# Expert down-projection weights: their loads moved from ScalarE's DMA queue to SyncE's

## The chip, the cores and the metric

The kernel runs on one core of one Trainium2 chip. The metric is the device time of one execution in microseconds. TensorE (PE), VectorE (DVE), ScalarE (ACT), GpSimd (POOL) and SyncE (SP) each run their own instruction stream and meet only at semaphores. Transfers are issued from SP's queue (q1 in the profile), ACT's (q10) or POOL's (q0), and all of them are carried by the core's 16 DMA engines.

## The reference

The kernel computes a decoder trunk of two layers on 512 tokens of width 1024 in float32. Layer 0 mixes tokens by dilated window attention, layer 1 by a gated DeltaNet; each mixer is followed by a mixture of experts (MoE), and each sub-layer is modulated by `c` and closed by a layer norm. What the change touches is the MoE:

```python
def swiglu(x, w1, w3, w2):
    return (jax.nn.silu(x @ w1) * (x @ w3)) @ w2

# 64 experts of hidden width 256; each token takes its 8 best, plus one shared expert
scores = jax.nn.sigmoid(xt @ router_w)
...                                   # group-limited top-8 on scores + router_bias -> eidx
gates = scores[eidx] / sum * 2.5
for each expert e:                    # rows grouped by expert
    y = swiglu(x[tokens of e], w1[e], w3[e], w2[e])
    acc[tokens of e] += y * gate
out = acc + swiglu(xt, ws1, ws3, ws2)
```

Per layer an expert has w1 and w3 (1 MiB each, the up weights) and w2 (1 MiB, the down weights), so the 64 experts weigh 192 MiB, and every one of them is read once per layer.

## The kernel before, in words

`build` runs the stages one after the other: setup, attention, MoE of layer 0, DeltaNet, MoE of layer 1. The two MoE stages (`moe_stage`) are built by the same code and take about 590 us each, from 834 to 1424 us and from 2100 to 2690 us of the profile.

A MoE stage routes the tokens, ranks the experts by how many tokens chose them, and then works through 45 **passes** of 128 gathered rows. A pass holds the rows of one to three experts: the three fullest experts first, one pass each, then a fixed mixture of experts with 96, 128 and 64 rows (`expert_passes`, L772). An expert's weights are one **load**; loads are numbered 0 to 63 in the order in which the passes need them, and `last_pass[n]` is the last pass that uses load n. Passes 7, 8, 9 are the last ones of loads 7, of 8 and 9, and of 10 and 11; pass 10 is the first to need loads 12 and 13, pass 11 load 14, pass 12 load 15, pass 13 load 16.

PE's stream for pass p is: index rows of pass p+3 (`rows_of`, L1720), the up-projection of pass p+1 (`up_of`, L1734, out into `moe_ph` or `moe_pr`), transposes (L1697, L1709), the down-projection of pass p (`down_of`, L1748, out into `moe_py`). ACT copies the result out (L1199), POOL scatters it to `y_rows` in HBM (L1269) and gathers the token rows of pass p+3 (L1265). Before `rows_of` of the next pass DVE must have written the scatter indices (L1458), for which it waits until an earlier scatter has landed.

Weights are held in **slots**: five for up weights, four for down weights. The up weights of load n go into the slot that load n-5 used, so their transfer waits for the up-projection of `last_pass[n-5]` (semaphore `h_done`, counted up by PE after L1734). The down weights of load n go into the slot of load n-4 and have to wait for the down-projection of `last_pass[n-4]` (`y_done`, after L1748). Loads 0 to 2 come ahead of the passes.

Who issues them sets the order. SP's program issues the up weights of loads 3 to 63 in a row (L1076, each with its `h_done` wait; L860, two transfers of 1 MiB). ACT's program issues the down weights (L863, one transfer of 1 MiB): load 3 once the order of the experts is known, the rest after the two copies L1199 of the pass whose down-projection freed the slot, without a wait of their own:

```python
for n in range(ew.EARLY + 1, NE):
    if last_pass[n - len(ew.DOWN_SLOTS)] == p:
        load_down(n)
```

Of the kernel before, what the change touches and what calls it, by code (L numbers as in the profile page):

```python
# [43 lines left out]
NE, TOPK, NG, TOPG = 64, 8, 8, 4  # L44
# [8 lines left out]
class Stage:  # L53
# [11 lines left out]
    def sem(self, name):  # L65
        s = self.ctx.enter_context(self.nc.semaphore(f"{self.tag}_{name}"))
        self.sems.append(s)
        return s
# [734 lines left out]
class ExpertWeights:  # L803
# [54 lines left out]
    def load_up(self, sp, e, slot, done):  # L858
        for a, src in enumerate(self.up_dram):
            sp.dma_start(self.up_slot(slot, a), src[:, bass.ds(e, 1)].rearrange("p a n -> p (a n)")).then_inc(done, 16)  # L860
# [21 lines left out]
def moe_stage(nc, c, A, l, ada_rows, h_rows, y_rows, ew, ring=None, out=None):  # L882
# [6 lines left out]
    passes, load_rank, last_pass = expert_passes()  # L889
# [4 lines left out]
    w13, w2, rw, rb, w13_in, w2_in, router_in = ew.w13, ew.w2, ew.rw, ew.rb, ew.w13_in, ew.w2_in, ew.router_in  # L894
# [38 lines left out]
    order = st.sb("order", [1, NE], I32)  # L933
# [40 lines left out]
    def vector(t):  # L974
        return t[norm // 2, norm % 2]
# [7 lines left out]
    def on_partitions(v):  # L983
# [20 lines left out]
    kth_ready, kth_turned, kthT_ready, rank_ready, ranked_done, order_ready = [  # L1004
        sem(x) for x in "kth_ready kth_turned kthT_ready rank_ready ranked_done order_ready".split()]
# [6 lines left out]
    y_done, y_ready = sem("y_done"), sem("y_ready")  # L1012
# [30 lines left out]
    with nc.Block() as block:  # L1043
        @block.sync
        def _(sp):
            for m, v in ((G, vector(A["ln_g"])), (B, vector(A["ln_b"])), (SHIFT, part(0)), (SCALE, part(1))):
                sp.dma_start(cols[:, m], v.rearrange("(p k) -> p k", k=KT)).then_inc(cols_in, 16)
            ew.load_early(sp)
            def store(t):
                sp.wait_ge(xn_ready, t + 1)  # L1050
                sp.dma_start(h_rows[t * P:(t + 1) * P, :], c.x[:, t]).then_inc(ew.h_out, 16)

            for t in range(TT - 1):
                store(t)
            sp.wait_ge(o_done, 2 * TT)
            ew.load_expert(sp, 2)
            store(TT - 1)
            sp.wait_ge(o_used, 2 * TT)
            sp.dma_start(c.ada[:, 2], spread(part(2))).then_inc(gate_in, 16)
            if not final:  # L1060
                for m, v in ((G, after[0]), (B, after[1]), (SHIFT, ada_rows[mod + 1, 0:D]), (SCALE, ada_rows[mod + 1, D:2 * D])):
                    sp.dma_start(next_cols[:, m], on_partitions(v)).then_inc(next_cols_in, 16)
            sp.wait_ge(order_ready, 1)

            def expert(n):
                return sp.value_load(order[0:1, load_rank[n]:load_rank[n] + 1], min_val=0, max_val=NE - 1)

            def load_up(n, e):
                slot, times = ew.up_place(n)
                if times == 1:  # L1070
                    sp.wait_ge(s_up, TT)
                else:
                    sp.wait_ge(h_done, last_pass[n - len(ew.UP_SLOTS)] + 1)
                ew.load_up(sp, e, slot, w13_in[slot])

            for n in range(ew.EARLY, NE):  # L1076
                load_up(n, expert(n))
            sp.wait_ge(h_done, max(last_pass[n] for n in range(NE) if ew.up_place(n)[0] == 0) + 1)
            sp.dma_start(shared_down.rearrange("p k d -> p (k d)"), A["shared_w2"][l].rearrange("(p k) n -> p (k n)", k=2))\
                .then_inc(s_down_in, 16)  # L1080
            sp.wait_ge(y_done, PASSES)

            def block(j):
                r = sp.value_load(ovi[0:1, bass.ds(j, 1)], min_val=0, max_val=NE - 1)
                e = sp.value_load(order[0:1, bass.ds(r, 1)], min_val=0, max_val=NE - 1)
                ew.load_up(sp, e, SPARE_UP, ov["w"])
                ew.load_down(sp, e, SPARE_DOWN, ov["w"])
                sp.wait_ge(ov["out"], 16 * j + 16)
                sp.sem_inc(ov["turn"], 1)

            further(sp, block)
            for b in range(2):
                sp.wait_ge(y_out[b], 16 * ((PASSES + 1 - b) // 2))
            for m in range(TT * PAIRS):
                t, pair = m // PAIRS, m % PAIRS
                if t >= 2 and pair < ON_PE // YG:
                    sp.wait_ge(d_done, t - 1)
                elif t >= 2:
                    sp.wait_ge(yg_used, 3 * (t - 2) + (1, 3)[pair - ON_PE // YG])
                sp.dma_start(yg[m % NYG], y_rows.rearrange("(t p k) d -> p t k d", p=P, k=TOPK)[:, t, pair * YG:(pair + 1) * YG])\  # L1100
                  .then_inc(yg_in[m % NYG], 16)
            if final:
                for t in range(TT):
                    sp.wait_ge(out_ready, t + 1)
                    sp.dma_start(out[0, t * P:(t + 1) * P, :], c.x[:, t]).then_inc(x_out, 16)
                sp.wait_ge(x_out, 16 * TT)
            else:
                ring.load_early(sp)
                for n in range(ring.slots):
                    sp.wait_ge(ring.w_in[n], 16)  # L1110

        @block.scalar
        def _(act):
# [48 lines left out]
                act.wait_ge(tx_done, 2 * p + 2)  # L1162
                modulated(p % 2).then_inc(xT_act, 1)

            def load_down(n):
                e = act.value_load(order[0:1, load_rank[n]:load_rank[n] + 1], min_val=0, max_val=NE - 1)
                slot, times = ew.down_place(n)
                ew.load_down(act, e, slot, w2_in[slot])

            keep_hidden(0)  # L1170
            silu_shared(1)
            keep_hidden(1)
            act.wait_ge(order_ready, 1)
            load_down(ew.EARLY)
            silu_shared(2)
            turned(0)
            keep_hidden(2)
# [6 lines left out]
            for p in range(PASSES):  # L1184
                act.wait_ge(th_done, p + 1)
                nc.scalar.copy(hT2[:, p % 2], th[:]).then_inc(hT_ready, 1)  # L1186
                if p + 2 < PASSES:
                    turned(p + 2)
                if p + 1 < PASSES:
                    silu(p + 1)  # L1190
                if p == 26:
                    act.wait_ge(route_ready, 1)
                    for n in range(2):
                        act.dma_start(c.ada[:, n], spread(after[n])).then_inc(next_in, 16)
                if p >= 2:
                    act.wait_ge(y_out[p % 2], 16 * (p // 2))
                act.wait_ge(y_done, p + 1)
                for n in range(2):
                    nc.scalar.copy(ysb[:, p % 2, half(n)], py[n][:]).then_inc(y_ready, 1)  # L1199
                for n in range(ew.EARLY + 1, NE):  # L1200
                    if last_pass[n - len(ew.DOWN_SLOTS)] == p:
                        load_down(n)
            act.wait_ge(y_out[0], 16 * ((PASSES + 1) // 2))
            act.wait_ge(y_out[1], 16 * (PASSES // 2))

# [1334 lines left out]
```

## Time and profile before

| | |
|---|---|
| median of 3 runs | 2762.76 us (2762.32 to 2770.57) |
| profiled execution, its own time | 2762.32 us |
| its span (first to last instruction) | 2760.6 us |
| PE busy | 2531.0 us (92%) |
| ACT busy | 674.9 us (24%) |
| DVE busy | 1016.3 us (37%) |
| DMA | 654.94 MB, mean 237 GB/s |
| mean granted TensorE clock | 0.969 |

How to read it: an engine's busy time is the union of its instructions. "Issue" in a wait stands for time in which the profile shows no semaphore as the cause, and a transfer whose semaphore was not matched is among these. The DMA share of a window is the mean busy share of the 16 DMA engines (it can read slightly over 1, because a packet is counted where it starts). Stretches of the two MoE stages are told apart by their time, since both have the same lines. In rows of the timeline SPq and ACTq mark what the sequencer of SP or ACT issued.

### The profile page before, as it was taken

The page shows a single profiled execution, that of the slowest core. Times are in us where ns is not written, and L with a number is a line of the kernel's source. Part 1 is how long each engine was busy: PE and PEld are TensorE (multiplying, and loading weights), DVE is VectorE, ACT ScalarE, POOL GpSimd, SP SyncE. Part 2 cuts the span into 40 slices and gives each one's busy share as a digit, 9 for nine tenths or more (in the row PEclk, how much of TensorE's full clock was granted, in tenths as well). Part 3 has the DMA queues.
Part 4 walks back from the last instruction along what each step waited for, and adds up shares of the span by engine and source line. Part 5 has one row for each costly group of instructions (what it writes and reads, how often), then busy time and mean ns, then how long its engine had stood idle before and what let it go on. Part 6 is the DMA issues. An engine that isn't in the chain of part 4 may idle for free. (4 is left out here: it accounts for less than half of the span.)

```text
span 2760.6 us, 37845 instructions
## 1 busy us (share of the span) xinstructions
PE 2531.0 (92%) x13849; PEld 1383.0 (50%) x13850; DVE 1016.3 (37%) x2302; ACT 674.9 (24%) x1468; POOL 337.1 (12%) x390
## 2 busy tenths in 40 slices
PE   6989989999899999989986999999799999899995
PEld 2665656656674443333332576675784434333332
DVE  2443344443453322311216444454444323222216
ACT  1031030310312222222212333334312222222221
POOL 0101001010001111111100121121101111111110
PEclk9999989999999999999998999999999999999998
DMA  7624326242528999999964131211356899999966
GB/s 276 187 62 146 97 76 197 62 141 86 216 102 318 355 421 420 413 410 405 416 250 166 43 92 38 83 46 60 115 202 241 330 420 420 405 416 417 407 255 275
DMA packets 177817, 654.94 MB, mean 237 GB/s; under 512 B 26885, under 2 KB 88685, under 8 KB 122505
## 3 DMA queue, kind: packets, MB, share of 16 engines
q1 hardware_dynamic: 112752, 394.89, 36.7%
q10 hardware_dynamic: 29784, 149.13, 14.2%
q0 software_dynamic: 35136, 109.10, 11.2%
q8 instruction: 80, 1.31, 0.2%
q14 instruction: 65, 0.52, 0.1%
HBM read 614.18 MB, written 53.52 MB: 242 GB/s over the span
## 5 line engine op out<-in xcount | busy, mean ns | idle before, releaser
L1462 DVE TENSOR_SCALAR core_oT<-moe_tx,moe_by,moe_plus 128x128 f32<-128x128 f32 x360 | 122.9, 403 | 666.8 <-PE moe_tx L1709 666.6
L675 PE MATMUL attn_proj<-core_hT,core_ring 128*128 128x512 f32 x768 | 339.4, 603 | 8.6 <-issue 5.2
L1734 PE MATMUL moe_ph<-weights_w,core_oT 128*32 128x512 f32 (+2 forms) x1216 | 313.0, 623 | 14.0 <-issue 14.0
L1748 PE MATMUL moe_py<-weights_w,moe_hT 128*32 128x512 f32 (+2 forms) x1296 | 312.7, 596 | 0.9 <-ACT moe_hT L1186 0.9
L1734 PE MATMUL moe_pr<-weights_w,core_oT 128*64 128x512 f32 (+2 forms) x864 | 271.1, 597 | 5.0 <-issue 5.0
L675 PEld LDWEIGHTS attn_proj<-core_hT,core_ring 128*128 128x128 f32 x768 | 148.3, 194 | 192.2 <-issue 191.8
L2395 PE MATMUL gdn_pj<-core_hT,core_ring 128*128 128x512 f32 x512 | 226.5, 597 | 0.0
L1269 POOL DMA_INDIRECT y_rows<-moe_ysb,moe_yidx x90 | 95.3, 1059 | 952.9 <-ACT moe_ysb L1199 698.3
L1186 ACT COPY moe_hT<-moe_th 128x256 f32<-128x256 f32 x90 | 33.6, 373 | 661.0 <-PE moe_th L1697 661.0
L671 PE MATMUL attn_proj<-core_ring,core_hT 128*128 128x256 f32 x768 | 176.5, 391 | 0.0
L671 PEld LDWEIGHTS attn_proj<-core_ring,core_hT 128*128 128x128 f32 x768 | 169.3, 282 | 11.2 <-issue 3.8
L2395 PEld LDWEIGHTS gdn_pj<-core_hT,core_ring 128*128 128x128 f32 x512 | 97.1, 192 | 117.5 <-issue 117.5
L1748 PEld LDWEIGHTS moe_py<-weights_w,moe_hT 128*32 128x32 f32 (+2 forms) x1296 | 92.4, 128 | 120.6 <-issue 113.3
L1734 PE MATMUL moe_ph<-core_ring,core_oT 128*32 128x512 f32 (+2 forms) x512 | 145.7, 621 | 5.8 <-issue 5.8
L1734 PEld LDWEIGHTS moe_pr<-weights_w,core_oT 128*64 128x64 f32 (+2 forms) x864 | 91.6, 140 | 117.6 <-issue 117.2
L1748 PE MATMUL moe_py<-core_ring,moe_hT 128*32 128x512 f32 (+2 forms) x416 | 145.4, 596 | 2.5 <-ACT moe_hT L1186 2.5
L1158 ACT ACTIVATE core_oT<-moe_tx,moe_plus,moe_by 128x128 f32<-128x128 f32 x360 | 135.3, 456 | 46.9 <-PE moe_tx L1709 46.9
L1734 PE MATMUL moe_ph<-core_hT,core_oT 128*32 128x512 f32 (+1 forms) x416 | 136.3, 646 | 7.9 <-issue 7.9
L1734 PEld LDWEIGHTS moe_ph<-weights_w,core_oT 128*32 128x32 f32 (+2 forms) x1216 | 87.6, 123 | 107.8 <-issue 107.4
L1199 ACT COPY moe_ysb<-moe_py 128x512 f32<-128x512 f32 x180 | 96.7, 589 | 172.5 <-PE moe_py L1748 172.5
L1265 POOL DMA_INDIRECT core_oT<-h_rows,moe_idx x90 | 90.8, 1009 | 121.3 <-DVE moe_yidx L1458 63.6
L1734 PE MATMUL moe_pr<-core_hT,core_oT 128*64 128x512 f32 (+2 forms) x224 | 100.7, 603 | 0.0
(410 smaller groups left out, 3438.7 us busy)
## 6 DMA issues: line engine op xcount, KB each, us to landing
weights_w<-in_expert_w_dram SPq DMA_DIRECT2D x160, 1024.0 KB, 15.3
weights_w<-in_expert_w_dram ACTq DMA_DIRECT2D x92, 1024.0 KB, 10.5
core_ring<-in_expert_w_dram SPq DMA_DIRECT2D x54, 1024.0 KB, 15.9
core_hT<-in_expert_w_dram SPq DMA_DIRECT2D x48, 1024.0 KB, 14.2
core_ring<-in_attn_w_in_dram SPq DMA_DIRECT2D x36, 1024.0 KB, 7.6
weights_w<-y_rows SPq DMA_DIRECT2D x32, 1024.0 KB, 13.3
core_ring<-in_expert_w_dram ACTq DMA_DIRECT2D x30, 1024.0 KB, 10.2
attn_ada_w<-in_ada_w_dram POOLq DMA_DIRECT2D x64, 384.0 KB, 6.0
```

Source lines behind the costliest of these rows:

```text
L671: last = nc.tensor.matmul(proj[n % 2][:, t % 2 * QF:(t % 2 + 1) * QF], c.hT[:, kk, toks], w[:, j % SLOTS, kk], start=kk == 0, stop=kk == K ...
L675: last = nc.tensor.matmul(proj[n % 2][:], w[:, j % SLOTS, kk, half_ * P:(half_ + 1) * P], c.hT[:, kk, :], start=kk == 0, stop=kk == KT - 1)
L1158: last = nc.scalar.activation(xT[:, b, k], tx[0][:, k], ACT.Identity, scale=by[:, k:k + 1], bias=plus[:, k:k + 1])
L1186: nc.scalar.copy(hT2[:, p % 2], th[:]).then_inc(hT_ready, 1)
L1199: nc.scalar.copy(ysb[:, p % 2, half(n)], py[n][:]).then_inc(y_ready, 1)
L1265: pool.indirect_dma_start(xg[:, b], None, h_rows, bass.IndirectOffsetOnAxis(ap=idx[:, b:b + 1], axis=0), bounds_check=SEQ - 1, oob_is_err= ...
L1269: pool.indirect_dma_start(y_rows, bass.IndirectOffsetOnAxis(ap=yidx[:, s:s + 1], axis=0), ysb[:, b], None, bounds_check=SEQ * TOPK - 1, oo ...
L1462: last = nc.vector.tensor_scalar(xT[:, b, k], tx[1][:, k - 4], by[:, k:k + 1], plus[:, k:k + 1], ALU.mult, ALU.add)
L1734: last = nc.tensor.matmul(ph[p % 2][at, :], xT[:, p % 2, k, at], w13[ew.up_place(n)[0]][:, :, k], start=k == 0, stop=k == KT - 1)
L1748: last = nc.tensor.matmul(py[n][at, :], hT2[:, p % 2, k, at], w2[ew.down_place(m)[0]][:, k, half(n)], start=k == 0, stop=k == 1)
L2395: last = nc.tensor.matmul(pj[h][:], w[:, n % 2, k, h * P:(h + 1) * P], c.hT[:, k], start=k == 0, stop=k == KT - 1)
```

## The change

SP's program now issues both kinds of weights. After the up weights of load n it issues the down weights of load n-1, behind a wait of its own for `y_done`; ACT no longer issues any. The number, the size and the place of the transfers stay as they are, as do the slots.

```diff
+            def load_down(n, e):
+                slot, times = ew.down_place(n)
+                if times > 1:
+                    sp.wait_ge(y_done, last_pass[n - len(ew.DOWN_SLOTS)] + 1)
+                ew.load_down(sp, e, slot, w2_in[slot])
+
+            e_before = None
             for n in range(ew.EARLY, NE):
-                load_up(n, expert(n))
+                e = expert(n)
+                load_up(n, e)
+                if e_before is not None:
+                    load_down(n - 1, e_before)
+                e_before = e
+            load_down(NE - 1, e_before)
...
-            def load_down(n):
-                e = act.value_load(order[0:1, load_rank[n]:load_rank[n] + 1], min_val=0, max_val=NE - 1)
-                slot, times = ew.down_place(n)
-                ew.load_down(act, e, slot, w2_in[slot])
-
             keep_hidden(0)
             silu_shared(1)
             keep_hidden(1)
-            act.wait_ge(order_ready, 1)
-            load_down(ew.EARLY)
...
-                for n in range(ew.EARLY + 1, NE):
-                    if last_pass[n - len(ew.DOWN_SLOTS)] == p:
-                        load_down(n)
```

SP, MoE stage of layer 0, kernel before: the up weights (L860) of loads 12, 13 and 14, each behind its own wait and, but for the first, whose reads stand ahead of the piece, behind the reads of the expert's number (L1066).

```order
L860 ISA [waits moe0_h_done]
L860 DMA core_ring<-in_expert_w_dram 128x2048 x2
L1066 TENSOR_LOAD moe_order
L1066 ISA x2
L860 ISA [waits moe0_h_done]
L860 DMA weights_w<-in_expert_w_dram 128x2048 x2
L1066 TENSOR_LOAD moe_order
L1066 ISA x2
L860 ISA [waits moe0_h_done]
L860 DMA core_hT<-in_expert_w_dram 128x2048 x2
```

The same place of SP's program in the changed kernel, up weights (L860) of loads 12, 13 and 14, with the down weights (L863) of loads 11 and 12 between them:

```order
L860 ISA [waits moe0_h_done]
L860 DMA core_ring<-in_expert_w_dram 128x2048 x2
L863 DMA weights_w<-in_expert_w_dram 128x2048 [waits moe0_y_done]
L1066 TENSOR_LOAD moe_order
L1066 ISA x2
L860 ISA [waits moe0_h_done]
L860 DMA weights_w<-in_expert_w_dram 128x2048 x2
L863 DMA weights_w<-in_expert_w_dram 128x2048 [waits moe0_y_done]
L1066 TENSOR_LOAD moe_order
L1066 ISA x2
L860 ISA [waits moe0_h_done]
L860 DMA core_hT<-in_expert_w_dram 128x2048 x2
```

What moved: between the up weights of two neighbouring loads there now stands one down transfer with a wait for `y_done`, so the second of them cannot be issued before that wait is over, even where its own slot is free.

ACT, MoE stage of layer 0, kernel before: from the second output copy of one pass (L1199) to the first copy of the next pass (L1186), with the down load that ACT issues between them.

```order
L1199 COPY moe_ysb<-moe_py 128x512
L1166 TENSOR_LOAD moe_order
L1166 ISA x2
L863 ISA
L863 DMA weights_w<-in_expert_w_dram 128x2048
L1186 COPY moe_hT<-moe_th 128x256 [waits moe0_th_done]
```

In the changed kernel (where these lines are L1204 and L1191):

```order
L1150 ACTIVATE moe_act_s<-moe_pr 128x256 [waits moe0_h_done]
L1204 COPY moe_ysb<-moe_py 128x512 [waits moe0_y_done]
L1204 COPY moe_ysb<-moe_py 128x512
L1191 COPY moe_hT<-moe_th 128x256 [waits moe0_th_done]
L1170 ACTIVATE core_oT<-moe_tx,moe_plus,moe_by 128x128 [waits moe0_tx_done]
```

What moved: the read of the expert's number, the register work and the down transfer are gone from ACT; the copy of the next pass follows the output copies at once.

## Rows read from the trace of the kernel before

**Rows 1.** Busy time and DMA share by stretch (us, engines, PEclk, DMA share, GB/s).
```profile
core 0: us, PE busy (x) PEld busy (x) DVE busy (x) ACT busy (x) POOL busy (x), PEclk, DMA share, GB/s
862.00:934.00 72.00, 71.86 (x447) 30.67 (x447) 23.86 (x64) 19.34 (x48) 12.12 (x12) 1.00 0.86 323
954.00:1090.00 136.00, 131.85 (x870) 54.13 (x863) 39.29 (x115) 34.38 (x86) 22.01 (x22) 1.00 1.01 420
1090.00:1340.00 250.00, 227.73 (x1469) 91.39 (x1469) 59.31 (x188) 58.31 (x145) 38.73 (x36) 0.97 1.00 410
2340.00:2600.00 260.00, 241.93 (x1556) 98.12 (x1555) 64.17 (x197) 61.85 (x154) 39.98 (x38) 0.97 1.00 411
```

**Rows 2.** Waits of PE in layer 0's MoE stage (us in total, times, longest).
```profile
PE moe_ph L1734 <- issue: 17.4, 4, 5.8
PE moe_pi L1715 <- DVE moe_yidx L1458: 11.1, 16, 1.9
```

**Rows 3.** Timeline of PE, the largest such idle time (start, us).
```profile
1192.83 1.08 PE L1734 MATMUL moe_ph<-core_hT,core_oT 128*32 128x512 f32 x3 [5.80 <-issue]
```

**Rows 4.** Timeline of PE: down-projections of passes 7, 8 and 9, up-projection of pass 10.
```profile
935.90 3.60 PE L1748 MATMUL moe_py<-weights_w,moe_hT 128*128 128x512 f32 x8
947.99 3.65 PE L1748 MATMUL moe_py<-weights_w,moe_hT 128*64 128x512 f32 x16
952.07 0.63 PE L1734 MATMUL moe_ph<-core_ring,core_oT 128*32 128x512 f32 x3
960.41 0.64 PE L1748 MATMUL moe_py<-core_ring,moe_hT 128*64 128x512 f32 x1
```

**Rows 5.** Timeline of SP: up weights of loads 12, 13, 14, then 15 and 16.
```profile
922.83 1.09 SPq L860 DMA_DIRECT2D core_ring<-in_expert_w_dram  x2
934.91 0.81 SPq L860 DMA_DIRECT2D weights_w<-in_expert_w_dram  x2
936.48 0.82 SPq L860 DMA_DIRECT2D core_hT<-in_expert_w_dram  x2
946.90 3.88 SPq L860 DMA_DIRECT2D weights_w<-in_expert_w_dram  x4
```

**Rows 6.** Timeline of ACT: copies out, down weights of load 11, of 12 and 13.
```profile
939.59 1.07 ACT L1199 COPY moe_ysb<-moe_py 128x512 f32<-128x512 f32 x2 [1.71 <-PE moe_py L1748]
940.29 0.34 ACTq L863 DMA_DIRECT2D weights_w<-in_expert_w_dram  x1
951.74 1.07 ACT L1199 COPY moe_ysb<-moe_py 128x512 f32<-128x512 f32 x2 [1.87 <-PE moe_py L1748]
952.46 1.39 ACTq L863 DMA_DIRECT2D weights_w<-in_expert_w_dram  x2
```

**Rows 7.** DMA queues, 936 to 954 us (packets, MB, share).
```profile
DMA packets 1215, 7.25 MB, mean 403 GB/s; under 512 B 280, under 2 KB 280, under 8 KB 383
q1 hardware_dynamic: 781, 5.75, 77.6%
q10 hardware_dynamic: 144, 1.05, 14.1%
q0 software_dynamic: 288, 0.42, 6.3%
```

**Rows 8.** Busy time by stretch: SP's queue alone, ahead of the MoE stage.
```profile
742.00:754.00 12.00, 12.00 (x61) 10.68 (x60) 4.69 (x9) 2.64 (x6) 0.00 (x0) 1.00 1.01 424
```

**Rows 9.** Issue to landing of the transfers of L860, of L863 and of L1269.
```profile
DMA to landing us min/median/max: 4.8/15.1/36.6
...
DMA to landing us min/median/max: 4.8/10.5/19.7
...
DMA to landing us min/median/max: 2.8/10.4/12.9
```

**Rows 10.** Layer 1, PE: down-projections of passes 7 and 8.
```profile
2201.84 3.60 PE L1748 MATMUL moe_py<-weights_w,moe_hT 128*128 128x512 f32 x8
2213.92 3.65 PE L1748 MATMUL moe_py<-weights_w,moe_hT 128*64 128x512 f32 x16
```

**Rows 11.** Layer 1, DMA queues, 2202 to 2220 us.
```profile
DMA packets 1206, 7.34 MB, mean 408 GB/s; under 512 B 241, under 2 KB 241, under 8 KB 382
q0 software_dynamic: 287, 0.58, 8.3%
```

## The prediction, made before the changed kernel had run

> **What bounds the kernel now.** I read the busy time by stretch first, then PE's waits, then the timeline where the loads start to fall behind. In a MoE stage the stretch table has two regimes [rows 1]. From 862 to 934 us PE is busy 71.86 of 72 us and the DMA engines move 323 GB/s at a share of 0.86: PE sets the pace, and the DMA engines stand idle 14% of the time, because no slot is free. From 954 us on the share is 1.01 at 420 GB/s, and from 1090 to 1340 us PE is busy only 227.73 of 250 us at an unchanged DMA share of 1.00: the transfers set the pace. PE's waits say the same: the up-projection (L1734) stood idle 17.4 us in 4 waits with no engine named, the longest 5.80 us at 1192.83 [rows 2, 3]; what it waits for there is up weights. The other wait, 11.1 us in 16 pieces, is for scatter indices, thus for a scatter that lands late [rows 2]. ACT is never the bound. So the question is what the change does to the moment at which the DMA engines become permanently busy, and to the bytes they then carry.
>
> **The bytes and the rate: no change.** All weights and all gathers stay. Could one queue be slower than two? Ahead of the MoE stage SP's queue alone filled the DMA engines: share 1.01 at 424 GB/s [rows 8], against 420 with three queues [rows 1]. I take 0 for this term, with a bound of 420 to 424 GB/s over the 450 us of a stage's saturated part, 4 us per layer as a gain and, with the 410 GB/s of the stretch in which PE waits, as much again as a loss.
> The Trainium skill's page "DMA: Bandwidth & Descriptors" states under "Issuing engines are not separate DMA queues" that transfers from SyncE, ScalarE and GpSimd run on the same 16 DMA engines and that several issuers only save issue time. By that rule, the rows agree, with 424 against 420 GB/s; taken alone it would make the whole change worth nothing, which is the first rival below.
>
> **What moves on ACT: nothing that is on the path.** ACT loses 61 issues per layer of 0.34 us each and as many reads of the expert's number. They stand behind the copies L1199 [rows 6], and ACT's next work waits for PE's transposes about 8 us later, so this is hidden before and the gain is 0 (at most 0.34 us times 45 passes, were it on the path, and no row puts it there). The down weights are issued up to 0.8 us earlier, since they no longer wait behind the first copy (down-projection of pass 7 ends at 935.90 + 3.60 = 939.5, ACT's issue is at 940.29 [rows 4, 6]). Their landings had room before, as no PE wait of L1748 for a transfer is in the rows: 0.
>
> **What moves on SP: up weights now wait for a down-projection.** Each up transfer n stands behind the down transfer of load n-2, which waits for the down-projection of the last pass of load n-6. PE does the up-projection of pass p+1 ahead of the down-projection of pass p, so this is later than the transfer's own condition. While PE sets the pace and buffers are deep, that costs nothing: those loads have tens of us to spare. The place where it costs is where the DMA engines go from idling to saturated, from about 935 us on. Load by load, layer 0 [rows 4 to 6]:
> - Up weights of load 13: before, issued at 934.91. Now behind the down weights of load 11, which wait for pass 7's down-projection: 939.5, so about 940.3 with the read of the expert's number between. 5.4 us later.
> - Up weights of load 14: before 936.48. Now behind the down weights of load 12, pass 8: 947.99 + 3.65 = 951.6, so about 952.5. 16 us later.
> - Load 15 (before 946.90) comes right behind it at about 954; load 16 waits for pass 9's down-projection, about 964.
>
> At 934.9 everything issued so far has landed in either kernel (load 12 was issued at 922.83), so both start level. Before, the 18 us from 936 to 954 moved 7.25 MB [rows 7]. Now the same 18 us hold: one down and two up transfers of 1.05 MB, 3.15 MB, issued from 939.6 on; the 0.42 MB of POOL's queue [rows 7]; and from about 953.2 (a lone transfer of 1.05 MB takes 4.8 us to land [rows 9] of which 2.5 us are bytes at 424 GB/s; I put 1.5 of the remaining 2.3 us ahead of the first byte) 0.8 us at 0.42 MB per us, 0.3 MB. Sum 3.9 MB. Missing: 3.35 MB, at 0.42 MB per us **8.0 us**. From there on the queue holds 6.3 MB (loads 12 and 13 down, 14 and 15 up), 15 us of work, and the next slots come at 964: the DMA engines are saturated in both kernels, so the deficit stays until the loads end.
> Layer 1: pass 7's down-projection ends at 2205.4, pass 8's at 2217.6 [rows 10]; the 18 us from 2202 moved 7.34 MB, 0.58 of it POOL's [rows 11]. Now 3.15 + 0.58 + 0.4 = 4.1 MB; 3.2 MB missing, **7.6 us**.
>
> **What is given back.** (a) In one queue the down weights no longer overtake: when the last late up weights (load 58) land, the down weights of 57 are still behind them, where before they shared the engines. Up to 1 MB, 2.5 us per layer; I take 1 us. (b) A scatter now shares the engines with one weight queue instead of two, and lands sooner than 10.4 us [rows 9], so the 11.1 us of index waits [rows 2] shrink. But where the DMA engines set the pace an earlier PE only waits longer for weights; the gain counts in the passes after the last late load alone, one wait of 0.9 us per layer. I take 1 us. The bounds of both together are 0 and 5 us per layer.
> The same page, under "Queues, rings and completion order", says each DMA engine alternates between the queues that have work; with one weight queue fewer the scatter would get a larger share. No run so far shows a scatter beside one saturated queue, and the sum above takes its gain from the rows only.
>
> **Sum.** 8.0 + 7.6 - 2 x 1 - 2 x 1 = 11.6 us on the profiled execution's own 2762.3 us (span 2760.6): 2773.9, say **2774 us**. That execution lies 0.4 us under the median of the runs shown, so no correction.
>
> **Rivals.**
> 1. *The wait is absorbed.* The up weights before arrived early in this stretch: PE's first real idle time comes much later than 954 us (busy 131.85 of 136 us until 1090 [rows 1]). If the DMA engines were not truly the bound after 1090, say because slots and not bytes hold them (share 1.00 but 410 instead of 420 GB/s [rows 1], 2.4% of 250 us = 6 us per layer), the order of need in one queue gives these 6 us back, and the result is 11.6 - 12 = about 0: 2762. For it: the rule above and the 410. Against it: the share is 1.00 throughout.
> 2. *The queue runs dry.* The opposite end, slower still. Up weights now get their slot one down-projection later throughout, so less is waiting in the queue. The loss of 10 GB/s between 1090 and 1340 us and between 2340 and 2600 us [rows 1] says engines already starve in part when PE has stalled, and a shorter queue could double that: 6 to 7 us per layer more, 2774 + 13 = 2787. It decides when the 3.15 MB issued at 939.6 need over 12.5 us to land (up-projection of pass 10 starts at 952.07 [rows 4]): then PE stalls already at pass 10, and each stall delays the next down-projection and by it the next load. By 424 GB/s they need 7.4 + 2.3 = 9.7 us; by the median landing of up weights, 15.1 us [rows 9], it would happen, but that median is of a queue with a backlog.
> 3. *Faster.* If besides rival 1 the early deficit does not reach the end, because the up weights then land in order instead of sharing the engines with down weights that have 10 us and more to spare: the 12 us of the 410 GB/s are gained and some of the slow clock after stalls (0.97 granted in the late stretches [rows 1]) with them: 2762 - 15 = 2747. Against it: 162 MB at 0.42 MB per us is what a layer has left after 934 us, and no order of the queue shortens that.
> That the change does not do what it says has no row for it: the order of SP's program shows the waits.
>
> **Chances.** Forecast 0.43 (its own range 2768 to 2780), rival 1 0.25, rival 2 0.20, rival 3 0.12. The range of all: 2756 to 2790. A measurement here can tell about 0.3%, 8.3 us, from no change: slower than 2771 is two thirds of the forecast and all of rival 2, 0.50, rounded up for stalls from pass 10 on to 0.52; faster than 2754 is rival 3, 0.12; the rest, 0.36, is within.
>
> **What the changed profile would show.** SP issues the up weights of load 13 at about 940 and of load 14 at about 952 on the same scale (5 and 16 us later than before); the 18 us behind pass 7 move about 4 MB instead of 7.25; a window from 970 to 1090 reads 420 GB/s again; PE's first waits of L1734 come earlier, around passes 14 to 16, instead of behind 1090 us; the waits for scatter indices shrink, and a scatter lands in less than 10 us; ACT's queue holds no expert weights. The stages before and between are unchanged. The forecast is wrong if the stretch between 936 and 954 moves as much as before, or if it does not and the two MoE stages still end at the old time: then the loads' bytes were not the bound.

## The result, and the profile after

| | before | changed |
|---|---|---|
| median | 2762.54 us (4 runs) | 2789.03 us (4 runs, 2785.49 to 2791.36) |
| ratio, 95% interval | | 1.0085 [1.0064, 1.0106] |
| profiled execution, its own time | 2762.32 us | 2787.23 us |
| its span | 2760.6 us | 2785.6 us |

The changed kernel is slower by 26.5 us of the medians. The time lies inside the stated range of 2756 to 2790 us, 1 us from its upper end, but outside the forecast's own range of 2768 to 2780; the forecast of 2774 us had less than half of the loss. In the profiled executions it is 24.9 us. First up-projection to last down-projection, layer 0's MoE stage takes 599.9 us instead of 587.7 (835.7 to 1435.6) and layer 1's 600.8 instead of 587.3 (2111.0 to 2711.8); together 1200.7 instead of 1175.0, 25.7 us more. Ahead of the first stage 0.9 us are added, the stretch between the two is 2.5 us shorter, and behind the second 0.9 us are added.

The rows that answer to [rows 1], then rows that follow pass 7 instead of the clock. For layer 0 these are: from 50 us ahead of the stage's first up-projection to 18 us behind the end of pass 7's down-projection; those 18 us alone; from there to the last down-projection. For layer 1 it is the first of the three.

```profile
862.00:934.00 72.00, 70.23 (x437) 30.48 (x437) 24.17 (x64) 19.34 (x48) 12.75 (x12) 1.00 0.85 320
954.00:1090.00 136.00, 128.47 (x866) 52.31 (x866) 37.86 (x113) 33.31 (x82) 21.17 (x21) 0.97 0.99 405
1090.00:1340.00 250.00, 230.87 (x1461) 92.73 (x1459) 58.57 (x186) 58.03 (x144) 37.65 (x38) 0.95 0.99 403
2340.00:2600.00 260.00, 239.65 (x1543) 96.58 (x1541) 62.53 (x193) 61.13 (x152) 38.72 (x38) 0.95 0.99 402
...
785.70:960.30 174.60, 170.47 (x924) 84.49 (x927) 65.19 (x223) 42.23 (x103) 25.10 (x23) 1.00 0.68 258
942.30:960.30 18.00, 17.96 (x135) 7.85 (x139) 4.49 (x14) 4.29 (x10) 4.03 (x4) 1.00 0.78 291
960.30:1435.60 475.30, 440.47 (x2767) 176.28 (x2756) 109.76 (x342) 111.61 (x277) 68.31 (x67) 0.96 0.97 393
2061.00:2235.90 174.90, 169.91 (x918) 83.88 (x920) 64.94 (x220) 42.23 (x103) 24.61 (x23) 1.00 0.70 264
```

The same stretches of the kernel before (the first of them ends 18 us behind its own pass 7):

```profile
784.80:957.50 172.70, 170.23 (x924) 83.80 (x926) 64.87 (x223) 42.24 (x103) 24.20 (x23) 1.00 0.74 281
939.50:957.50 18.00, 18.00 (x135) 7.51 (x139) 4.51 (x14) 4.30 (x10) 4.04 (x4) 1.00 1.01 414
957.50:1422.50 465.00, 433.00 (x2764) 174.25 (x2756) 111.10 (x342) 111.58 (x277) 70.14 (x67) 0.98 0.96 395
2050.40:2223.40 173.00, 170.22 (x925) 83.83 (x927) 64.55 (x220) 42.24 (x103) 24.18 (x23) 1.00 0.76 286
```

Until 18 us behind pass 7 the kernel before has moved 172.7 us x 281 GB/s = 48.5 MB, the changed one 174.6 x 258 = 45.0: 3.5 MB less, in layer 1 49.5 - 46.2 = 3.3 MB less. That is the deficit that the prediction worked out as 3.35 and 3.2 MB. Its own window, 936 to 954 us [rows 7], begins 3.5 us ahead of pass 7's end. The same window of the changed kernel moves 18 x 230 = 4.1 MB where 3.9 were forecast, instead of 7.25:

```profile
938.80:956.80 18.00, 17.96 (x112) 7.86 (x114) 7.43 (x21) 6.07 (x15) 2.42 (x3) 1.00 0.62 230
```

Where it is made, SP's timeline shows (start, us; answers to [rows 5]): down weights of load 11, up of 13, down of 12, up of 14.

```profile
942.31 0.33 SPq L863 DMA_DIRECT2D weights_w<-in_expert_w_dram  x1
943.39 0.81 SPq L860 DMA_DIRECT2D weights_w<-in_expert_w_dram  x2
954.46 0.33 SPq L863 DMA_DIRECT2D weights_w<-in_expert_w_dram  x1
955.55 0.81 SPq L860 DMA_DIRECT2D core_hT<-in_expert_w_dram  x2
```

Pass 7's down-projection ends at 942.3 here. The up weights of load 13 leave 1.1 us behind it and those of load 14 13.3 us; forecast were 0.8 and 13.

What SP waited for in layer 0's stage, kernel before, then changed kernel (us in total, times, longest): before, the waits for PE's projections at these loads stood at an up load (L860); now nearly all stand at a down load (L863), and the up weights behind it find their own slot already free.

```profile
SPq L860 <- PE moe_ph L1734: 227.1, 20, 17.4
SPq L860 <- PE moe_pr L1734: 215.2, 21, 20.9
```
```profile
SPq L863 <- PE moe_py L1750: 448.1, 42, 18.6
```

PE's waits in layer 0's MoE stage, then in layer 1's (answers to [rows 2]):

```profile
PE moe_pr L1736 <- issue: 20.9, 5, 5.6
PE moe_ph L1736 <- issue: 12.1, 5, 3.4
PE moe_pi L1717 <- DVE moe_yidx L1460: 1.7, 2, 0.9
```
```profile
PE moe_pr L1736 <- issue: 18.9, 5, 4.8
PE moe_ph L1736 <- issue: 14.0, 7, 3.5
PE moe_pi L1717 <- DVE moe_yidx L1460: 2.3, 4, 1.1
```

The kernel before, beside [rows 2]: one more row of layer 0, then layer 1.

```profile
PE moe_pr L1734 <- issue: 1.7, 2, 1.5
```
```profile
PE moe_pi L1715 <- DVE moe_yidx L1458: 13.9, 16, 1.7
PE moe_ph L1734 <- issue: 10.3, 4, 3.5
PE moe_pr L1734 <- issue: 3.3, 1, 3.3
```

The waits for indices have gone from 11.1 to 1.7 us and from 13.9 to 2.3, and yet the kernel is slower: PE waits for up weights instead, 33.0 us in layer 0 against 19.1, and 32.9 us in layer 1 against 13.6. The first of these waits in layer 0 is ahead of pass 15:

```profile
1021.53 1.09 PE L1736 MATMUL moe_pr<-core_hT,core_oT 128*64 128x512 f32 x1 [5.63 <-issue]
```

What follows it, by stretch (columns as in [rows 1]; the last two figures are DMA share and GB/s, ahead of them the granted clock):

```profile
1022.00:1025.00 3.00, 3.00 (x9) 0.82 (x7) 0.00 (x0) 0.00 (x0) 0.00 (x0) 0.50 1.02 423
1025.00:1028.00 3.00, 3.00 (x11) 0.96 (x9) 0.00 (x0) 0.00 (x0) 0.00 (x0) 0.57 1.02 421
1028.00:1031.00 3.00, 3.00 (x17) 1.08 (x14) 0.00 (x0) 0.00 (x0) 0.00 (x0) 1.00 1.01 421
...
1034.00:1037.00 3.00, 3.00 (x27) 1.04 (x23) 1.29 (x7) 0.85 (x4) 0.00 (x0) 1.00 0.64 270
```

Two things follow a stall. PE comes back at 0.50 of its clock, the 1.2 GHz level, after 5.6 us without work, and so loses about 3 us more in that up-projection. And at 1034 us the DMA engines run dry (share 0.64): SP stands at the `y_done` wait of a down load until 1036.55, while PE has yet to do a whole down-projection. By PE's account layer 0's 12.2 us are 13.9 us more of waiting for up weights, 9.4 less for indices, and the remaining 7.7 are PE's own work, which took longer at a lower granted clock (behind pass 7 PE is busy 440.47 us instead of 433.00, at 0.96 instead of 0.98).

Landings (min/median/max) of L863, L860 and L1271, the lines of [rows 9]:

```profile
DMA to landing us min/median/max: 4.7/13.3/20.0
...
DMA to landing us min/median/max: 4.8/14.9/24.9
...
DMA to landing us min/median/max: 2.6/8.9/11.1
```

### The profile page after: what moved, and what is told of

The parts are those of the page before. It is cut to its first block and busy times, and to the rows that moved or that the text cites. A ratio compares the mean times of both kernels' runs of the same rounds, so it can differ in the third digit from the quotient of the medians.

```text
span 2785.6 us, 37355 instructions
## 1 busy us (share of the span) xinstructions
PE 2543.8 (91%) x13849; PEld 1389.2 (50%) x13850; DVE 1014.0 (36%) x2302; ACT 675.2 (24%) x1468; POOL 335.2 (12%) x390
## 3 DMA queue, kind: packets, MB, share of 16 engines
q0 software_dynamic: 35136, 109.10, 11.1%
## 5 line engine op out<-in xcount | busy, mean ns | idle before, releaser
L1736 PE MATMUL moe_ph<-weights_w,core_oT 128*32 128x512 f32 (+2 forms) x1216 | 303.5, 604 | 13.1 <-issue 13.1
L1736 PE MATMUL moe_pr<-weights_w,core_oT 128*64 128x512 f32 (+2 forms) x864 | 294.0, 630 | 22.9 <-issue 22.5
L1271 POOL DMA_INDIRECT y_rows<-moe_ysb,moe_yidx x90 | 93.4, 1038 | 982.4 <-ACT moe_ysb L1204 875.5
L1191 ACT COPY moe_hT<-moe_th 128x256 f32<-128x256 f32 x90 | 33.6, 374 | 686.1 <-PE moe_th L1699 686.1
L1204 ACT COPY moe_ysb<-moe_py 128x512 f32<-128x512 f32 x180 | 96.6, 589 | 173.0 <-PE moe_py L1750 173.0
L1736 PE MATMUL moe_ph<-core_hT,core_oT 128*32 128x512 f32 (+1 forms) x416 | 128.9, 607 | 6.1 <-issue 6.1
L1736 PE MATMUL moe_pr<-core_hT,core_oT 128*64 128x512 f32 (+2 forms) x224 | 109.9, 648 | 10.4 <-issue 10.4
```

The costliest lines, as they stand in the source:

```text
L1271: pool.indirect_dma_start(y_rows, bass.IndirectOffsetOnAxis(ap=yidx[:, s:s + 1], axis=0), ysb[:, b], None, bounds_check=SEQ * TOPK - 1, oo ...
L1736: last = nc.tensor.matmul(ph[p % 2][at, :], xT[:, p % 2, k, at], w13[ew.up_place(n)[0]][:, :, k], start=k == 0, stop=k == KT - 1)
```

## Experiments

Each ratio is to runs of the kernel before beside it on the same chip (e1 to e4 share one chip, e5 to e8 a second, e9 to e11 a third); 0.001 is 2.8 us, and the intervals are some 3 to 6 us wide on either side. The last column is the time of the two MoE stages together, first up-projection to last down-projection, in the one profiled execution of each. Outside them all kernels do the same work, and yet that rest differs by up to 12 us between these executions (layer 0's stage begins at 829.8 us in e5 and at 841.3 in e7). So for a small effect the column says where it lies.

"Turns" are the change's order: up weights of load n, then down weights of load n-1. In the cuts of code below the numbers of slots are written out, and `...` stands for lines left out.

| kernel | median us | ratio [95%] | both stages, us |
|---|---|---|---|
| before | | 1 | 1175.0 |
| the change | 2789.03 | 1.0085 [1.0064, 1.0106] | 1200.7 |
| e1 two queues, wait alone | 2803.56 | 1.0144 [1.0122, 1.0166] | 1218.0 |
| e2 one queue, down two behind | 2764.83 | 1.0005 [0.9996, 1.0015] | 1173.8 |
| e3 one queue, order of freed slots | 2770.34 | 1.0024 [1.0011, 1.0036] | 1183.0 |
| e4 turns to load 16, then e3's order | 2791.95 | 1.0098 [1.0081, 1.0115] | 1202.0 |
| e5 e3's order to 16, then turns | 2773.95 | 1.0043 [1.0030, 1.0056] | 1188.9 |
| e6 one queue, order of need | 2762.97 | 0.9997 [0.9983, 1.0011] | 1172.6 |
| e7 load 3 first, e3's order to 16, then e2's | 2758.50 | 0.9986 [0.9975, 0.9998] | 1169.1 |
| e8 the change, down 3 first | 2792.80 | 1.0108 [1.0094, 1.0123] | 1200.8 |
| e9 turns to load 11, then e3's order | 2777.85 | 1.0044 [1.0030, 1.0057] | 1185.6 |
| e10 turns for loads 12 to 16 alone | 2786.09 | 1.0072 [1.0057, 1.0087] | 1197.5 |
| e11 e3's order to 16, then need | 2754.81 | 0.9964 [0.9950, 0.9978] | 1165.0 |

**Wait or queue (e1, e3, e2).** e1 is the kernel before with the wait and without the move:

```diff
                     sp.wait_ge(h_done, last_pass[n - len(ew.UP_SLOTS)] + 1)
+                    if n - 2 >= len(ew.DOWN_SLOTS):
+                        sp.wait_ge(y_done, last_pass[n - 2 - len(ew.DOWN_SLOTS)] + 1)
```

> The kernel before, its down weights still issued by ACT on its own queue; only the wait is added: SP waits for the down-projection of the last pass of load n-6 ahead of the up weights of load n, as the change makes it do. Theory W (the change loses its 26.5 us because up weights are held back behind a wait for a down-projection): all of the loss is here, 2782 to 2792 us, and the DMA engines run dry at 940 to 956 us of layer 0 and again behind each of PE's stalls. Theory Q (the one queue and its order of bytes is what costs, the wait is absorbed): 2760 to 2766. Scatters stand beside two weight queues as before: they land in 10.4 us by both, and PE's waits for scatter indices stay over 8 us per layer unless the longer stalls cover them.

It is slower than the change itself, and than theory W's range: the wait alone holds all of the loss and more. Its layer 0 shows where the rest goes: on two weight queues the waits for indices stay, and grow. With its waits for up weights, 25.7 us, they sum to 47.0 (in an execution 8 us over e1's median), against 34.7 in the changed kernel.

```profile
PE moe_pi L1717 <- DVE moe_yidx L1460: 21.3, 20, 3.2
PE moe_ph L1736 <- issue: 8.0, 3, 3.5
```
```profile
DMA to landing us min/median/max: 2.6/10.7/13.0
```

Scatters (second fence, L1271) land in 10.7 us beside two weight queues and in 8.9 beside one. With the same waits for slots, the kernel with one queue is 2803.6 - 2789.0 = 15 us faster (16 by the ratios, some 8 either way). The two kernels also differ in who issues the down weights and in the order in which weights land; that the shorter landings of scatters make the 15 us is argued from the waits for indices, not shown alone.

e3 is the change with the loads sorted by the moment at which PE frees their slots:

```diff
+            freed = [(2 * last_pass[n - 5] - 1 if n >= 5 else -9, n, load_up) for n in range(3, NE)]
+            freed += [(2 * last_pass[n - 4] + 2 if n >= 4 else -8, n, load_down) for n in range(3, NE)]
+            freed.sort(key=lambda f: f[:2])
+            for _, n, load in freed:
+                load(n, expert(n))
```

> The changed kernel with all expert weights on SP's queue, but issued in the order in which PE frees their slots (up weights of load n after the up-projection of load n-5's last pass, down weights after the down-projection of load n-4's last pass, merged by PE's program order), so that no transfer stands behind a wait that ends later than its own. Theory W: the loss is gone, 2756 to 2766 us. Theory Q: the single queue costs still, 2780 or more. By both the scatters land in less than 9 us as in the changed kernel (8.6 against 10.4), and PE's waits for scatter indices are under 5 us per layer against 11.1 and 13.9 before; if that were worth time by itself, W gives 2756 rather than 2762.

Nearly all of the loss is gone, but 6 to 8 us stay, more than the wait theory gave. PE's largest waits there, layer 0:

```profile
PE moe_py L1747 <- DMA weights_w<-in_expert_w_dram: 17.0, 5, 6.3
PE moe_py L1747 <- DMA core_ring<-in_expert_w_dram: 15.6, 3, 6.8
```

They are at the down-projection (L1747). This order puts the down weights of load m behind the up weights of load m+2, and for 35 of the 61 loads of m+3 too, which PE needs later (e2, below, stops at m+2); the down weights take 16.6 us (median) from issue to landing, where they took 10.5 on ACT's queue. So the one queue has an effect of either sign: scatters land sooner, and down weights can come late.

e2 issues the down weights of load n-2 behind the up weights of n:

```diff
-                    load_down(n - 1, e_before)
...
+                    load_down(n - 2, held.pop(0))
...
```

> The changed kernel with the down weights one turn later: after the up weights of load n SP issues the down weights of load n-2 instead of n-1, so the up weights of load n stand behind the down-projection of load n-7's last pass instead of n-6's, which is over when their own slot comes free in most turns. Theory W: most of the loss is gone, 2758 to 2770 us, a bit above the merged order where the down wait still ends last. Theory Q: 2780 to 2790 as the change, since the queue is the same. A third outcome, above 2790, would say that down weights now land too late and PE waits at the down-projection (L1750 or its like with a DMA as releaser), which W alone doesn't give.

One place in the order gives all of it back: the same queue, the same transfers, a time within theory W's range that its interval can't tell from the kernel before. The waits for down weights of the third outcome didn't come.

**Where in the stage (e4, e5, e9, e10).** These take the turns of the change for some loads and e3's order for the rest; the order is split by load number:

```diff
+            def stretch(n, load):
+                k = n + (load is load_down)
+                return 0 if k <= 11 else 1 if k <= 16 else 2
+            for k, order_of in enumerate((merged, turns, merged)):      # e10; e9: turns, merged, merged
+                for n, load in [x for x in order_of if stretch(*x) == k]:
+                    load(n, expert(n))
```

> The changed kernel's turns (up n, down n-1) for up weights to load 16 and down weights to load 15 alone, the merged order of freed slots from there on. It prices the first term of the prediction by itself: the DMA engines that run dry once per layer, when they go from idling to saturated (forecast 8.0 and 7.6 us less 2 x 2 us given back, 11.6 us in all). If that term was right and the rest of the 26.5 us comes from dry spells behind PE's later stalls (13 us in all): 2768 to 2778 us. If the early deficit is the whole loss: 2784 to 2791. If the early deficit is caught up later: 2758 to 2765.

It is 1 us above the range in which the early deficit is the whole loss: the early turns alone cost 0.74% over e3, 20 us (19.0 in the stages), where the first term was 15.6 less 4 given back. The time is as high as the change's.

> The other half of the split: the merged order of freed slots up to up weights 16 and down weights 15, the changed kernel's turns (up n, down n-1) from there on. Merged throughout gave 2770.3 us, turns early and merged late 2792.0, turns throughout 2789.0. Theory E (the whole loss is made where the DMA engines go from idling to saturated, and nothing is lost later): 2764 to 2771 us, the merged kernel's time less up to 6 us, because with turns PE no longer waits for down weights late in the stage. Theory R (each of PE's stalls costs a dry spell again, 1 to 3 us of idle DMA engines at 1034, 1115 and 1281 us of the changed kernel): 2776 to 2784. By E these dry spells are there before PE's stalls only because the deficit has made PE stall; by R they come back here.

Between the two theories: 0.19% over e3, 5 us (medians 3.6, stages 5.9), above the one range and below the other. But e3 pays for late down weights in this very part. Against the kernel before, the late turns of e5 cost 0.43%, 12 us (13.9 in the stages). And the costs of the two parts don't add: the early turns cost 0.74% ahead of e3's late order (e4 over e3), and 0.42% ahead of late turns (the change over e5).

> The early part of the changed kernel's turns cut in two, first half: turns (up n, down n-1) for up weights to load 11 and down weights to load 10 alone, which are issued while PE sets the pace and the DMA engines idle; the merged order from there on (merged throughout: 2770.3 us, turns to up weights 16: 2792.0). The prediction put these loads at nothing, since they have tens of us to spare: 2768 to 2773 if that holds. The changed kernel's pass 7 ended 1.9 us later after the stage's start than before (106.6 against 104.7 us), and its DMA engines idled 17.1 instead of 13.6 us until then: if that stays to the end, 2 x 2 to 2 x 3.5 us more than merged, 2774 to 2778. Above 2780 would make this half the larger one.

0.20% over e3, 5.6 us by the ratios and 7.5 by the medians. In the profiled executions only 2.6 us of it lie in the two stages (3.3 more in layer 0, 0.7 less in layer 1); the rest lies outside them, where this order changes nothing. So by the traces no more than about 3 us can be put down to the order. The prediction had nothing here. This kernel's layer 0 (stage's start to pass 7, then the 18 us behind it) against e3's, which stand second:

```profile
841.00:947.60 106.60, 104.58 (x568) 46.85 (x567) 35.08 (x93) 26.86 (x68) 16.86 (x15) 1.00 0.88 337
947.60:965.60 18.00, 18.00 (x135) 7.45 (x137) 4.44 (x14) 4.30 (x10) 4.04 (x4) 1.00 1.02 421
```
```profile
834.50:939.10 104.60, 104.03 (x566) 46.12 (x565) 34.65 (x93) 26.86 (x68) 15.29 (x15) 1.00 0.91 345
939.10:957.10 18.00, 18.00 (x135) 7.48 (x138) 4.39 (x14) 4.30 (x10) 4.04 (x4) 1.00 1.01 413
```

The first row of each: PE needs 106.6 instead of 104.6 us for passes 0 to 7 (in layer 1 105.3 instead of 104.5), while the 18 us behind it are as full as e3's, and the bytes moved until then are the same 43.5 MB. The loss here is that PE is late, not that bytes are missing.

> The second half: turns for up weights 12 to 16 and down weights 11 to 15 alone, the loads whose waits the prediction followed one by one (up weights of loads 13 and 14 held back to 940 and 952 us), the merged order before and behind. The term was forecast at 8.0 and 7.6 us: 2770.3 + 15.6 = 2786, or 2784 to 2788, if the deficit stays to the end. By the bytes measured (2.2 MB less in the 18 us behind pass 7 than in the merged kernel, 5.3 us at 0.415 MB per us): 2781. Below 2775 would say that a deficit made in this place alone is caught up, and that the whole early part needs the first half too.

0.48% over e3: 13.3 us by the ratios, 15.8 by the medians, 14.5 in the stages, beside the 15.6 of the forecast. Its layer 0 (from 50 us ahead of the stage to 18 us behind pass 7), and e3's:

```profile
789.40:962.00 172.60, 170.28 (x925) 83.83 (x927) 64.88 (x223) 42.24 (x103) 24.20 (x23) 1.00 0.69 260
```
```profile
784.50:957.10 172.60, 170.27 (x925) 83.85 (x927) 64.83 (x223) 42.24 (x103) 24.20 (x23) 1.00 0.74 281
```

172.6 us x 21 GB/s = 3.6 MB less, 8.7 us at the 414 GB/s that the kernel before moves behind this stretch; the stage is 7.1 us longer than e3's, and layer 1's is 7.4 us longer. The early loss splits into e9's 5.6 and e10's 13.3 us by the ratios, which sum to 19, as e4 has 20; in the stages it is 2.6 and 14.5, as e4 has 19.0.

**One transfer earlier (e8).** 

```diff
+            load_down(ew.EARLY, expert(ew.EARLY))
             for n in range(ew.EARLY, NE):
...
```

> The changed kernel's turns with one transfer moved: the down weights of load 3 ahead of all up weights instead of behind those of load 4 (their slot has been free all along, while the up weights wait for the shared expert). At the first up-projection of a MoE stage the changed kernel had moved 1.0 MB of weights less than the one before, 1.0 / 0.42 = 2.5 us of full rate. If that deficit lasts to the end as the one at 942 us does: 2 x 2.5 = 5 us less than the changed kernel, 2782 to 2786. If it is made up while the DMA engines still idle (they idle 17 us of the first 107): 2788 to 2790.

No gain: 2792.8 us is above both ranges, and the two stages take 1200.8 us where the change's take 1200.7. The megabyte is there at the start of layer 0's stage (in the 50 us ahead of it 121 GB/s against 100) and is gone 18 us behind pass 7 (174.4 us x 258 GB/s = 45.0 MB, as in the change). Banked while the DMA engines idle anyway, it bought nothing.

**A better order (e6, e7, e11).** e6 sorts by need (`first_pass[n]` is the first pass that uses load n); e11 takes e3's order for up weights to load 16 and down weights to load 14, and e6's from there:

```diff
+            needed = [(2 * first_pass[n] - 1, n, load_up) for n in range(3, NE)]
+            needed += [(2 * first_pass[n] + 2, n, load_down) for n in range(3, NE)]
+            needed.sort(key=lambda f: f[:2])
```

> All expert weights on SP's queue in the order in which PE needs them: the up weights of a pass's loads ahead of the down weights of the pass before, by first pass of each load. The wait theory says: the up weights stand behind down-projections that are over by then in most turns, as in the run with the down weights one turn later (2764.8); in the first passes (up weights of loads 8 to 13) the waits stand in each other's way more than there. 2760 to 2772 us. If order of need is what counts and the early idle time of the DMA engines is no longer than in the merged order: 2756 to 2762, with PE's waits at both projections under 35 us in both layers together.

> One queue with what the runs so far favour in each part: the down weights of load 3 first, then the merged order of freed slots to up weights 16 and down weights 14 (no dry spell at 940 to 956 us), and from there on up n, down n-2 (the order with the lowest time so far, 2764.8, whose only dry spell was 2.8 us at 949 to 953). If the deficits add up as DMA idle time over 420 GB/s: 2764.8 less 2 to 3 us per layer for the dry spell and up to 2.5 per layer for load 3: 2754 to 2761, under the kernel before. If one of them is made up elsewhere: 2761 to 2765, no difference.

> One queue again, for the best version: the merged order of freed slots to up weights 16 and down weights 14, then the order of need (the up weights of a pass's loads ahead of the down weights of the pass before). Order of need throughout gave 2763.0, with 16.8 and 14.7 us of idle DMA engines before pass 7's end; merged has 10.8 and 9.5 there, and the run of merged first and down weights two behind later gave 2758.5. If early idle time counts: 2755 to 2760. If it doesn't (the slots, not the order, limit what is banked before the saturated part): 2761 to 2764.

Order of need throughout (e6) equals the kernel before, within its first range; PE's waits at both projections are 51 us, not under 35, and its DMA engines stay idle longer ahead of pass 7. e7 is faster than before by 0.14%, just clear of its interval and within its first range, and e11 by 0.36%, 8.9 us of the medians (10.0 in the stages), at its expectation's low end: it beats both kernels. e11's layer 0 from 18 us behind pass 7 on, beside [rows 1] and the 465.00 us of the kernel before:

```profile
961.90:1422.60 460.70, 433.71 (x2764) 174.76 (x2756) 109.61 (x342) 111.78 (x277) 68.11 (x67) 0.97 0.97 399
```

It has the full rate at the start of the saturated part from e3 (its 18 us read 409 GB/s), no waits for down weights, and the short landings of scatters (8.6 us): layer 0 has 1.1 us of waits for indices left of 11.1, and 24.0 us for up weights where the kernel before has 19.1. The three come together here; none was taken away by itself.

## Why the prediction fell short, step by step

The mechanism was right: bytes not issued at the edge of the saturated part. The size was short by 14 us of the 25.7 that the two stages lost. By the account below, 0.9 us of them are in the deficit, 3.7 in the loads ahead of pass 7, and 9.5 in what is given back, where 4 us were to be gained and 5.5 were lost. That the time lies in the range is due to the price of rival 2, whose mechanism was met in part only; to that extent it is luck.

- **What bounds the kernel, right.** Bytes that are late at the start of the saturated part stay late to the end. e10 shows it alone, ahead of e3's late order: of 8.7 and 8.3 us of missing bytes, 7.1 and 7.4 are left at the end of the stages. With late turns less of it is left: the change is 4.3 and 7.4 us longer than e5 in the two stages.
- **The deficit behind pass 7, right in place and size.** 3.35 and 3.2 MB were worked out, 3.5 and 3.3 MB measured; 8.0 + 7.6 us forecast, 8.5 + 8.0 from the bytes measured, 13 to 16 us in e10.
- **Loads ahead of pass 7 at nothing, wrong.** "While PE sets the pace and buffers are deep, that costs nothing" is the first step that failed. In the changed kernel pass 7 ends 106.6 us after the stage's start instead of 104.7, in layer 1 106.9 instead of 105.1, 3.7 us in both, and e9 prices the turns there at about as much (2.6 us in the stages, 5.6 by the ratios). The time is lost in short waits for indices ahead of passes 2 and 5. The trace shows what stands beside the late scatter: in the changed kernel SP issues one down and two up transfers, 3.1 MB, between 855.7 and 857.6 us, and the scatter issued at 857.62 lands after 10.6 us; before, a single down transfer left ahead of it (855.55), the next up weights at 862.33, and it landed after 6.3. That the bunch delays it wasn't tried by itself.
- **What is given back, wrong in sign of the net.** Forecast 2 us gained per layer; behind the deficit 1.8 us are lost in layer 0 and 3.7 in layer 1. The end of the stage does give back more than that: between 1379.5 and 1422.5 us the kernel before has a DMA share of 0.53, thus 20.2 us idle, the changed one in its last stretch 13.3:

```profile
957.50:1379.50 422.00, 392.59 (x2538) 158.97 (x2534) 106.58 (x328) 102.05 (x254) 65.15 (x62) 0.98 1.01 414
1379.50:1422.50 43.00, 40.41 (x234) 15.28 (x223) 4.51 (x15) 9.53 (x23) 4.99 (x5) 1.00 0.53 202
```
```profile
960.30:1382.30 422.00, 388.90 (x2470) 156.60 (x2459) 102.77 (x320) 98.86 (x246) 61.31 (x60) 0.96 0.99 405
1382.30:1435.60 53.30, 51.56 (x299) 19.68 (x297) 6.99 (x22) 12.75 (x31) 7.00 (x7) 1.00 0.75 303
```

  But the 422 us ahead of it (first fence before, second changed) run at 405 instead of 414 GB/s: 3.8 MB, 9.2 us, in dry spells behind PE's stalls as the one at 1034. 9.2 lost and 6.9 returned leave 2.3 us lost where 2 were to be gained. That the dry spells behind stalls cost this is read from one trace; no run takes them away alone.
- **Layer 0 in sum:** 1.9 ahead of pass 7, 8.5 of deficit (3.5 MB at 414 GB/s), about 2 of dry spells less the end: 12.4, measured 12.2. Layer 1: 1.8, 8.0, and 3.7 left over: 13.5. The forecast was 6.0 and 5.6.
- **The scatter, right in direction.** Landing 8.9 instead of 10.4 us in the median, index waits nearly gone. Cited for this was the Trainium skill's page "DMA: Bandwidth & Descriptors", section "Queues, rings and completion order", that an engine alternates between the queues with work: e1 and the change have the same waits on two weight queues and on one, and agree with it, 10.7 against 8.9 us. I had said that an earlier PE would only wait longer for weights. In the change it did (9.4 us less for indices, 13.9 more for up weights in layer 0), but e1, which has the wait and two queues, is 15 us slower still.
- **Rival 1, the wait absorbed: refuted** by e1 and e10. The rule of the Trainium skill's page behind it ("DMA: Bandwidth & Descriptors", section "Issuing engines are not separate DMA queues") isn't: moving the transfers between queues without the wait costs 0.24% (e3) and, in a better order, nothing (e2, e6). The loss was in SP's program order, which that rule doesn't speak of.
- **Rival 2, the queue runs dry: the number of 2787 was met, the mechanism in half.** Dry spells recur, but its point of decision failed: PE waited under 0.1 us ahead of pass 10 in layer 0 and 0.6 in layer 1, and its first long stall is at pass 15. Late turns alone (e5) cost 12 us over the kernel before, close to its 13, but only 5 over e3; and they don't add to the early ones.
- **Rival 3, faster: not for this order.** A gain is there all the same, 9 us in e11, for the one queue and a better order together; the order was not tried on two queues.
- **Signs named ahead:** issue times right, measured from the end of pass 7, which itself came 2.8 us later by the clock; 970 to 1090 us at 420 GB/s again wrong (it reads 411, a dry spell lies in it; before 421); first waits around passes 14 to 16 right; about 4 MB instead of 7.25 right for the window meant, 4.1 MB. (It was called the 18 us behind pass 7, but begins 3.5 us ahead of its end; the 18 us truly behind it moved 5.2 MB against 7.5.) "The stages before and between are unchanged" holds to 0.9 and 2.5 us.

## What to carry to other kernels

A wait put into a shared instruction stream is paid by what is queued behind it: compare, load by load, the moment at which the transfer's own condition is met with that of the wait ahead of it, and look first at the point where the DMA engines go from idling to saturated, since most of the bytes not issued there were missing to the end here. When loads of two kinds share one queue, their order matters: here the best was by freed slot while the engines still idled and by need once they were saturated. And a wait that disappears (21 of 25 us for indices here) is no gain by itself if another wait limits the same stretch. To price a part of a change, compare the stretch that it touches as well as the whole time: e9's 5.6 us were 2.6 there.

## What was not expected of the hardware

- With unchanged waits, the kernel with one weight queue instead of two was 15 us faster (e1 against the change): scatters landed in 8.9 instead of 10.7 us, gathers in 10.9 instead of 12.8. Early in the stage it was the other way round: a scatter issued right behind 3.1 MB of weights took 10.6 us, where it had taken 6.3 behind one transfer of 1.05 MB.
- One stall of PE costs twice: after 5.6 us without work the granted clock read 0.50 for the next 3 us and 0.57 for the 3 after, at a DMA share of 1.02. With longer stalls at weights PE's busy time behind pass 7 rose by 7.5 us in layer 0 and 5.7 in layer 1, for the same work.
